# A recurrent update on VectorE or a third chunk on TensorE: the sample tokens of a gated DeltaNet layer

## The reference, cut to what matters

```python
S = S * exp(g_t); kv = k_t @ S                     # sample tokens, one by one
S = S + outer(k_t, (v_t - kv) * b_t); o_t = q_t @ S
o = rmsnorm(o, norm_w) * silu(z)                   # both kinds of tokens
```

## Time and profile before

| | |
|---|---|
| time, median of 3 runs | 2902.24 us (2901.11 to 2912.59) |
| the profiled execution | 2906.3 us, span 2904.3 us |
| mean granted TensorE clock | 0.918 |
| busy: PE, DVE, ACT, POOL | 2579.0, 1751.0, 1083.1, 1654.3 us |
| span by stretches: prologue; GDN loop; last GDN pass | 0 to 135; 135 to about 1304; to about 1388 us |
| granted clock in the GDN loop; in the output projection after it | 0.88; 1.00 |
| chain that ended last, first two shares | issue 35%, POOL 30% |

### The profile page before, as it was taken

One profiled execution on the slowest core, in us unless ns is written; L12 is line 12 of the kernel. 1 busy time (PEld: TensorE's weight loads), 2 busy tenths in 40 slices (PEclk: granted clock), 3 DMA queues, 4 the chain that ended last, 5 costly groups with the idle time before them and its releaser, 6 DMA issues.

```text
span 2904.3 us, 58389 instructions
## 1 busy us (share of the span) xinstructions
PE 2579.0 (89%) x21022; PEld 2378.3 (82%) x21022; DVE 1751.0 (60%) x3882; ACT 1083.1 (37%) x1752; POOL 1654.3 (57%) x2236
## 2 busy tenths in 40 slices
PE   6888889889888898898999898788988899799998
PEld 5877888778778787887999898777977788699987
DVE  5767667676776766767321415777777676823242
ACT  5433333333333333333333434343433434433343
POOL 4534434343444443433788676566755676597765
PEclk8988889889888898988999998999999999899999
DMA  4333333233333322333545345446654565264433
GB/s 179 117 117 118 130 117 117 89 115 116 117 117 117 131 96 95 121 112 116 187 152 176 103 155 194 155 150 202 209 168 139 187 219 182 100 214 143 155 116 119
DMA packets 126773, 410.86 MB, mean 141 GB/s; under 512 B 21344, under 2 KB 37984, under 8 KB 122112
## 3 DMA queue, kind: packets, MB, share of 16 engines
q1 hardware_dynamic: 81216, 295.75, 30.3%
q10 hardware_dynamic: 45504, 114.38, 11.3%
HBM read 363.47 MB, written 46.61 MB: 141 GB/s over the span
## 4 chain that ended last, share of the span: by engine, by line
issue 35%; POOL 30%; PE 22%; DVE 11%; ACT 2%; DMA 0%; POOLq 0%; ACTq 0%; DVEq 0%
POOL wl L313 30%; PE psj L336 6%; PE psj L338 6%; PE psj L337 6%; DVE arena L1271 4%; DVE arena L1269 2%; DVE arena L1561 1%; ACT arena L1109 1%; PE psA L676 1%; PE psE L343 1%; PE psE L631 1%; DMA arena<-s_rows_d 0%; DVE arena L1634 0%; DVE arena L1632 0%; PE psA L343 0%
## 5 line engine op out<-in xcount | busy, mean ns | idle before, releaser
L313 POOL TENSOR_TENSOR wl<-ring,wh 128x256 fp32r<-128x256 f32 x2232 | 1654.1, 777 | 1227.3 <-ACT wh L727 1226.4
L336 PE MATMUL psj<-xh,wh 128*128 128x288 f32 x4400 | 1416.7, 322 | 49.0 <-DVE xl L1208 20.0
L337 PE MATMUL psj<-xl,wh 128*128 128x288 f32 x4400 | 1335.4, 304 | 0.0
L338 PE MATMUL psj<-xh,wl 128*128 128x288 f32 x4400 | 1329.4, 302 | 0.0
L336 PEld LDWEIGHTS psj<-xh,wh 128*128 128x128 f32 x4400 | 861.9, 196 | 135.4 <-issue 99.4
L337 PEld LDWEIGHTS psj<-xl,wh 128*128 128x128 f32 x4400 | 865.4, 197 | 8.5 <-issue 3.9
L338 PEld LDWEIGHTS psj<-xh,wl 128*128 128x128 f32 x4400 | 863.6, 196 | 0.0
L727 ACT ACTIVATE wh<-ring 128x1024 fp32r<-128x1024 f32 x558 | 564.5, 1056 | 241.3 <-PE psj L338 214.8
L1271 DVE SCALAR_TENSOR_TENSOR arena<-arena 128x256 f32<-128x256 f32 (+1 forms) x672 | 325.0, 549 | 2.6
L795 ACT ACTIVATE arena<-psj 128x256 f32<-128x256 f32 x112 | 42.9, 383 | 403.1 <-PE psj L338 401.0
L1542 DVE TENSOR_TENSOR arena<-Y,arena 128x288 f32<-128x288 f32 x32 | 14.6, 458 | 163.1 <-ACT arena L988 162.4
(11 more groups left out here) (283 smaller groups left out, 3097.3 us busy)
## 6 DMA issues: line engine op xcount, KB each, us to landing
ring<-weights_d SPq DMA_DIRECT2D x558, 512.0 KB, 3.3
h<-gstate_d ACTq DMA_DIRECT2D x16, 1024.0 KB, 7.3
gst_s_d<-h ACTq DMA_DIRECT2D x16, 1024.0 KB, 3.9
h<-sstate_d ACTq DMA_DIRECT2D x32, 512.0 KB, 6.4
sst_s_d<-h ACTq DMA_DIRECT2D x32, 512.0 KB, 5.1
arena<-g_rows_d ACTq DMA_DIRECT2D x16, 864.0 KB, 4.5
arena<-s_rows_d ACTq DMA_DIRECT2D x8, 1152.0 KB, 9.8
h_spill_d<-h ACTq DMA_DIRECT2D x2, 2304.0 KB, 7.8
```

Of the source, the lines that this page charges most:

```text
L313: ins = pool.tensor_tensor(wl[:, s, n:n + 2], ring[:, s, n:n + 2], wh[:, s, n:n + 2].bitcast(F32), ALU.subtract)
L336: pe.matmul(out, w_h, xh[:, kt, :], start=(kt == 0), stop=False)
L337: pe.matmul(out, w_h, xl[:, kt, :], start=False, stop=False)
L338: mm = pe.matmul(out, w_l, xh[:, kt, :], start=False, stop=(kt == KT - 1))
```

## The change

The 32 sample tokens become a third chunk of the chunked rule, with the mask "same sequence, and token not later". The sample part on VectorE is replaced by small products on TensorE, and outputs of both kinds come out with tokens on partitions, so that the norm's sum runs along the columns of one partition.

- TensorE, step 0: k^T k and k^T q of the sample tokens (psE) instead of a transpose. Step 3: two transposes of k spread by sequence, and the read-out of the states as 16 products of 256 columns, k into rows 0 to 31 and q into rows 32 to 63 of psD. Steps 6, 7, 10: the inverse of the 32 x 32 matrix from two factors. Step 19: the sample v to tokens. Step 23: the new values, step 27: the outputs. Step 31: all eight updates of the states, in four banks. Step 36: six transposes of the normed outputs (psE, psF), after g_on. Step 39: the sums for the next q and k, in psA and psB.
- `gdn_ready(m, e)` holds three waits ahead of the projection of a step: g_as before step 6, g_bs before step 10, the scaled new values before step 27.
- VectorE: the exponents of pairs, pair products and `gdn_sample` go. New are the masks of k and q by sequence, some operations on 32 x 32, the row sum of squares (768 columns), the scaling of outputs (g_on), and the two products to Y, which now stand among the updates of the states.
- ScalarE: the decay exponents of GDN and of SSD as Relu of (cumulated g of the column's token as a bias, minus the row), with scale -1 in the Exp; squares out of PSUM; one root of 6 columns; the roots of the next q and k stand ahead of the stores of the states.
- Prologue: a few masks, 20 small products, one copy more.

The diff, cut to its core:

```diff
+            def gdn_ready(m, e):
+                if e == 6:
+                    pe.wait_ge(S("g_as"), m + 1)
+                if e == 10:
+                    pe.wait_ge(S("g_bs"), m + 1)
+                if e == 27:
+                    pe.wait_ge(S("g_sample_act"), m * 4 + SMP_ACT["vnds"])
...
                 if e == 3:
-                    pe.wait_ge(S("g_pr"), m + 1)
-                    col_sum(psD[:, 0:2 * NPAIR], ga["PR"])
+                    pe.wait_ge(S("g_mk"), m + 1)
+                    for r in range(2):
+                        mm = pe.transpose(psF[:, r * P:(r + 1) * P], gMK[:, 4 * r:4 * r + 4, :], ident)
+                    mm.then_inc(S("g_sample_pe"), 1)
                     pe.wait_ge(S("g_st_in"), m * 16 + 16)
                     for b in range(DEC_B):
-                        for j in range(2):
-                            at = 160 + 16 * b + 8 * j
-                            mm = halves(psD, slice(at, at + 8), gS[:, b, j, :], gKN[:, 0:2, SEQ + b:T:DEC_B])
-                    mm.then_inc(S("g_smp"), 1)
+                        for n in range(2):
+                            mm = pe.matmul(psD[NS * n:NS * n + NS, 0:2 * P], (gMK, gMQ)[n][:, b, :], gS[:, b, :, :],
+                                           start=(b == 0), stop=(b == DEC_B - 1))
+                    mm.then_inc(S("g_sample_pe"), 1)
...
+                if e == 31:
+                    pe.wait_ge(S("g_sample_act"), m * 4 + SMP_ACT["kmc"])
+                    pe.wait_ge(S("g_ot"), m + 1)
+                    for r in range(2):
+                        for g in range(4):
+                            rows = slice(NS * g, NS * g + NS)
+                            mm = pe.matmul((psA, psB, psC, psD)[g][:, r * 256:(r + 1) * 256], gKM[rows, r, :],
+                                           gVNDS[rows, :], start=True, stop=True)
+                    mm.then_inc(S("g_sp"), 1)
+                if e == 36:
+                    pe.wait_ge(S("g_on"), m + 1)
+                    for j in range(2):
+                        for c in range(NC):
+                            at = j * SEQ + c * CH
+                            pe.transpose(psE[:, at:at + CH], gON[:, 2 * c + j, :], ident)
+                    for j in range(2):
+                        mm = pe.matmul(psF[:, NS * j:NS * (j + 1)], gON[NS:2 * NS, 4 + j, :],
+                                       ident[NS:2 * NS, NS:2 * NS], start=True, stop=True)
+                    mm.then_inc(S("g_ont"), 1)
+                if e == 39 and more:
+                    pe.wait_ge(S("g_su"), m * 4 + 2)
                     gdn_norm(m + 1)
...
 (ScalarE, start of a pass)
-                act.activation(ga["DT"], ga["DT"], ACT.Exp)
-                act.activation(ga["DEC"], ga["DEC"], ACT.Exp).then_inc(S("g_dte"), 1)
+                for c in range(NC):
+                    for j in range(2):
+                        act.activation(gDT[:, 2 * c + j, :], gR[:, j, 0, c * CH:(c + 1) * CH], ACT.Relu,
+                                       bias=gcc[:, 1, c, j:j + 1], scale=-1.0)
+                for j in range(2):
+                    ins = act.activation(gDTS[:, j, :], gR[:, j, 0, SEQ:T], ACT.Relu, bias=gscc[:, 1, j:j + 1],
+                                         scale=-1.0)
+                ao.link(ins)
+                act.activation(ga["DT"], ga["DT"], ACT.Exp, scale=-1.0).then_inc(S("g_dte"), 1)
...
 (VectorE, in the inversion: level lv)
                     if lv < CONV_W:
                         v_tap(lv)
+                    if lv == 1:
+                        dve.wait_ge(S("g_sample_pe"), m * 7 + SMP_PE["sqs"])
+                        dve.tensor_tensor(gBS[:, :, :], bc(ident[0:NS, 0:NS], 1, 2),
+                                          psD[0:NS, 256:256 + 2 * NS].rearrange("p (j t) -> p j t", j=2), ALU.add) \
+                            .then_inc(S("g_bs"), 1)
...
 (VectorE, end of a pass; states(g) updates the sequences g and 4 + g)
+                dve.wait_ge(S("g_osq"), m + 1)
+                dve.tensor_reduce(ga["OS"], gSQO[:, :, :], AXIS.X, ALU.add).then_inc(S("g_oss"), 1)
+                dve.wait_ge(S("g_sp"), m + 1)
+                states(0)
+                dve.wait_ge(S("g_rs2"), m + 1)
+                do.link(dve.reciprocal(ga["OR"], ga["OR"]))
+                dve.tensor_tensor(gON[:, 0:4, :], psF[:, :].rearrange("p (u t) -> p u t", u=4),
+                                  bc(ga["OR"][:, 0:4], 2, P), ALU.mult)
+                dve.tensor_tensor(gON[NS:2 * NS, 4:6, :], gOT[:, :, :], bc(ga["OR"][NS:2 * NS, 4:6], 2, P), ALU.mult) \
+                    .then_inc(S("g_on"), 1)
+                states(1)
...
 (ScalarE, SSD layer, before each of the two Exps)
+                    for hh in range(HPG):
+                        ins = act.activation(sDT[:, hh, :], sR2[:, hh, c * CH:(c + 1) * CH], ACT.Relu,
+                                             bias=scc[:, 1, c, hh:hh + 1], scale=-1.0)
```

More of the change, by code:

```diff
@@ L20 @@
 ACT = mybir.ActivationFunctionType
+AXIS = mybir.AxisListType
 P = 128
@@ L77 @@
 N_PRM = C_SND + 2 * SX * SG
-G_DVE_LINKS, S_DVE_LINKS = 34, 27
+SMP_PE = {n: i + 1 for i, n in enumerate(("kmt", "smp", "ast", "sqs", "esp", "us", "osm"))}
+SMP_ACT = {n: i + 1 for i, n in enumerate(("kmc", "asc", "qs", "vnds"))}
+G_DVE_LINKS, S_DVE_LINKS = 19, 27
 ARENA = 15900
@@ L446, in gdn_mix @@
                     new_values(0)
+                if e == 23:
+                    pe.wait_ge(S("g_es"), m + 1)
+                    pe.wait_ge(S("g_rss"), m + 1)
+                    for j in range(2):
+                        mm = pe.matmul(psA[:, j * P:(j + 1) * P], gES[:, j, :, :], gVBS[:, j, :], start=True, stop=True)
+                    mm.then_inc(S("g_sample_pe"), 1)
                 if e == 24:
@@ L508, in _ @@
                 for c in range(NC):
-                    src = HRG[0:GV, (7, 3, 4, 5)[n], c * CH:(c + 1) * CH]
+                    src = HRG[0:GV, (7, 6, 4, 5)[n], c * CH:(c + 1) * CH]
                     at = (n * NC + c) * GV
                     mm = pe.transpose(psD[:, at:at + GV], src, ident[0:GV, 0:GV])
+            for n in range(5):
+                src = HRG[0:GV, (7, 6, 4, 8, 5)[n], SEQ:T]
+                for g in range(4):
+                    mm = pe.matmul(psD[NS * g:NS * g + NS, 256 + n * GV:256 + (n + 1) * GV], src, ident[0:GV, 0:GV],
+                                   start=True, stop=True)
             mm.then_inc(S("g_ccol"), 1)
@@ L892, in gdn_body @@
                         u = 2 * c + j
[L893 to L894 removed]
+                        act.activation(gVB[:, u, :], psB[:, u * P:(u + 1) * P], ACT.Copy,
+                                       scale=gcc[:, 0, c, j:j + 1])
+                for j in range(2):
+                    ins = act.activation(gVBS[:, j, :], psE[0:NS, 256 + j * P:256 + (j + 1) * P], ACT.Copy,
+                                         scale=gscc[0:NS, 0, j:j + 1])
                 ins.then_inc(S("g_vb"), 1)
@@ L1437, in gdn_body @@
                 less_q(1, 5)
-                dve.wait_ge(S("g_cv"), m + 1)
-                for piece in range(1, 6):
-                    gdn_sample(piece, m)
+                dve.wait_ge(S("g_sample_pe"), m * 7 + SMP_PE["smp"])
+                dve.wait_ge(S("g_vb"), m + 1)
+                dve.wait_ge(S("g_dtx"), m + 1)
+                for j in range(2):
+                    ins = dve.scalar_tensor_tensor(gVBS[:, j, :], psD[0:NS, j * P:(j + 1) * P], gscc[0:NS, 2, j:j + 1],
+                                                   gVBS[:, j, :], ALU.mult, ALU.add)
+                ins.then_inc(S("g_rss"), 1)
                 if not full:
@@ L1459, in gdn_body, with states @@
                     take_out(T_O1, 1)
-                for i in range(4):
-                    dve.wait_ge(S("g_sp"), m * 4 + i + 1)
-                    for b in (2 * i, 2 * i + 1):
+                def states(g):
+                    bank = (psA, psB, psC, psD)[g]
+                    for r in range(2):
+                        b = 4 * r + g
                         for j in range(2):
-                            at = (b % 2) * 256 + j * P
+                            at = r * 256 + j * P
                             ins = dve.scalar_tensor_tensor(gS[:, b, j, :], gS[:, b, j, :],
@@ L1477, in gdn_body @@
                     .then_inc(S("g_y"), 1)
+                states(2)
+                states(3)
                 if full:
```

281 lines of the change are left out of this document (135 added, 146 removed).

## The result

The changed kernel takes **2821.45 us** (median of 4 runs, 2816.62 to 2824.59) against 2901.99 (4 runs) for the kernel before: ratio 0.9716, 95% interval 0.97 to 0.9732. The profiled execution took 2822.21 us, span 2820.4, mean granted clock 0.95. The forecast was 2830, the range 2765 to 2905: the time lies in it, and "faster by over 0.5%" had the chance 0.66.

The account below looks back on a forecast made before the run. TensorE's in-order queue, with its waits and the lower clock behind them, was taken to bound the kernel. 79.4 against 84.03 us a pass, 15 times, is -69; with -9 SSD and +1.5 prologue, 2906.3 becomes 2829.8, said as 2830 (2765 to 2905).

Parts of the forecast that it names:

- Part I: Steps 31 to 0 of a pass, 29.45 us before: 17.3 work, 2.2 wait, 2.0 clock, 21.5 us (19.5 to 24).
- The term of 2.0 for the clock: Behind the wait for normed outputs at step 36: 2.0 us lost to a lower clock, between bounds 0 and 4.3.
- The prediction's own bracket: How long TensorE may wait: clock kept at 1.00 after a 2.56 us wait, 0.67 after 2.75.
- Part II: Steps 0 to 7 of a pass, 17.53 us before, claimed to become 13.7 us (11.8 to 17.5).
- Part III: Steps 7 to 31, 37.05 us before, to become 44.2 us (40 to 46), with 3.7 wait before step 10.
- the signs that were to show it: Waits: step 10, 3 to 4 us; step 36, 2 to 3; step 6, about 1; Part III clock under 0.95.
- four signs of being wrong: Clock 1.00 after step 10; wait there under 1 us; read-out 7 us; normed outputs over 9 us after step 31.
- SSD: SSD layer: exponents leaving VectorE remove waits of 1.14 us a group, 9 us gained in all (0 to 12).
- (a): Clock kept after both new waits, at steps 36 and 10: 83 us less, 2747; chance 0.12.
- (b): Clock low for a whole stretch after both new waits, steps 36 and 10: 54 us more, 2884; chance 0.16.
- (c): Read-out of the states: two 32-wide tiles don't overlap as four do, +3.85 a pass, 58 us, 2888; chance 0.07.
- (d): Normed outputs for step 36 come late, 14.4 us instead of 8.2: 128 us more, 2958; chance 0.13.

Follow-up runs that it names:

- run 9: Changed kernel with the BS products at step 12 instead of 10 and state stores ahead of the next q/k roots, read-out still at step 3: 2725.77 us, ratio 0.9393.
- run 5: Kernel before, with the GDN prompt decay exponents as Relu on ScalarE and VectorE's pair products ahead of the sample-pair exponents: 2822.2 us, ratio 0.9726.
- run 3: Changed kernel with ScalarE's stores of the states ahead of the next q and k roots: 2792.05 us, ratio 0.9625.
- run 8: Changed kernel with BS products at step 12, state stores ahead of the next roots, and the read-out of the states at step 5: 2742.59 us, ratio 0.9434.
- run 1: Changed kernel with the wait for g_bs and its two small products moved from step 10 to step 12: 2750.42 us, ratio 0.9484.
- run 2: Changed kernel with the SSD layer's decay exponents back on VectorE, GDN untouched: 2833.98 us, ratio 0.9769.
- run 6: Changed kernel with the 16 read-out products reordered, all keys and then all queries instead of in turn: 2856.89 us, ratio 0.9839.
- run 4: Kernel before, with only the GDN prompt decay exponents moved to ScalarE as Relu: 2863.56 us, ratio 0.9866.
- run 10: run 9 with the transposes of the normed outputs at step 38 instead of 36 and VectorE's last state updates earlier: 2707.32 us, ratio 0.9331.
- run 7: Changed kernel with the read-out of the states moved from step 3 to step 17: 2873.38 us, ratio 0.9895.

## Why the prediction was right, step by step

**Part I** (21.5 predicted, 19.80 measured). The wait for the normed outputs: predicted 2.2, since g_on at 8.2 and TensorE ready at 6.0; measured 1.70, with g_on 8.0 us after step 31 and TensorE ready at 6.3. The work without a wait was predicted as 17.3 and is 18.10, 0.8 too little. The term of 2.0 for the clock was wrong in this pass: it stayed at 1.00. So -0.5 - 2.0 + 0.8 = -1.7: two errors hide a third. In run 9 both occur, behind 1.70 and 1.69 us of the same wait:

```profile
361.90:372.00 10.10, 10.08 (x72) 9.67 (x73) 8.33 (x17) 3.15 (x6) 3.43 (x5) 1.00 0.50 183
434.10:444.20 10.10, 10.09 (x60) 9.58 (x61) 6.88 (x17) 3.15 (x6) 1.99 (x3) 0.83 0.54 184
```

0.17 of 10.1 us is 1.7 lost in one pass and nothing in another. The size 2.0 was about right for a pass in which it happens; in the changed kernel it happens in 3 of 15, which makes 0.3 a pass. The prediction's own bracket had put this wait on the side that is kept, and against it I took the 2.0. The bracket itself (kept behind 2.56, lost behind 2.75) did not hold either: the clock was lost behind 1.69 in run 9, and kept over 9 us behind 2.40 in run 5.

**Part II** (13.7 predicted, 17.28 measured): the largest error. At full clock the read-out takes 3.65 us (run 3; predicted 3.85), but in the changed kernel the clock falls inside it: 17.28 x 0.10 = 1.7, a loss that the prediction had put at nothing here. The states land later than I counted, so that the wait was 2.34, not 1.0 (+1.3): the load took 8.7 us from issue to landing (median of the 16), where the earlier trace rows have 6.7 in the pass that I read. The wait of 0.95 for the masked keys I had missed; VectorE, which masks them, waits itself for the rows of g, that leave the same queue:

```profile
DVE arena L1404 <- DMA arena<-g_rows_d: 53.7, 16, 3.7
```

 The wait of 0.9 for g_as did not come, as TensorE was later by all of this; in run 8, where it was not, it is there, 0.90 us. 13.7 + 1.7 + 1.3 + 0.95 - 0.9 = 16.8 of 17.3. Run 3 shows the queue as the cause of most: with the stores first, 2 us a pass come back.

**Part III** (44.2 predicted, 42.45 measured). The wait for g_bs was predicted as 3.7 and is 3.71 us; run 1 takes it away. The clock cost 42.45 x 0.04 = 1.7, not 3.5: it fell only after the wait was over and was low for about 3.4 us (0.62 in the first 3.05 us, 0.85 in the next 3.5). That both old waits of 1.1 us would go was right, and so were the 2.2 for products and copies as a whole: 37.05 - 2.2 + 3.7 + 1.7 + 2.2 = 42.45. (Three times the 0.61 of the earlier trace rows are 1.8, not 1.7 with two tiny products on top.)

The errors of the three parts, -1.7, +3.6 and -1.7, cancel to +0.1 (79.53 in this pass against 79.4). The total was right to 0.3% partly by luck; of the four waits that came I had three in the right place and two in about the right size, and a fifth did not come; of the clock behind them I had only the loss at step 10, at twice its size. Of the signs that were to show it, these came otherwise: the wait before step 36 is 1.70 and not 2 to 3 us, there is none before step 6, parts I and II are 9.9 and not 12 us shorter, and part III has a clock of 0.96, where I wanted under 0.95. None of the four signs of being wrong came. **SSD**: 9 predicted, 12.5 measured (run 2), since the wait is longer than 1.14 in one group (5.0). **Prologue**: 1.5 and 1.1.

**The rivals.** (a) the clock kept after both waits: half true, it was kept at step 36 in 12 of 15 passes and lost at step 10 in all. (b) low for a whole stretch: no. (c) 32-wide tiles that don't overlap: excluded by the 3.65 us of run 3; run 6 shows what it would have cost. (d) g_on late: excluded, 8.0 us. The Trainium skill's rule that relu belongs on VectorE ("ScalarE: Activation LUTs", Rules for kernel authors) did not pay here: the move to ScalarE gained 38 us in the kernel before (run 4), and the way back cost 12.5 in the SSD layer (run 2). The Relus of 128x128:

```profile
404.63 1.28 ACT L926 ACTIVATE arena<-arena 128x128 f32<-128x128 f32 x4 [0.45 <-DVE arena L1407]
```

0.32 us each, against 0.74 on VectorE beside GpSimd. Alone VectorE needs 0.28 (the median of L1561), so one instruction for one the rule is not refuted; what decided was whose queue the work stood on. Relu needed no table load of its own: the one of 1.28 stands ahead of the first Relu, from 402.89, while ScalarE waits for VectorE anyway, and serves the Exp as well.

**What stays open.** Why the clock falls in one pass and not in the next behind the same wait. Behind the 3.7 us of the changed kernel it fell each time, in the pass read 0.7 us later; behind 2.31 in run 4 it fell, behind 2.40 in run 5 it did not, and behind 0.53 with 0.90 in run 8 it did both. The length of a wait does not decide it alone. No run takes part I apart, the largest gain of all: how much of it is the state products, the norm's sums or the order of the queue is not shown.

## What to carry to other kernels

Where one engine runs a written-out order, price a change by what stands on that engine's queue, and try the order first: moving existing work gave 71, 29 and 18 us (runs 1, 3, 10) and 41 us in the old kernel (run 5 against run 4), beside 80 for the change of method, and busy totals of the other engines told nothing. Price each wait twice, its own length and the clock that may fall behind it, and don't count a removed wait before looking at the one that it hid (runs 5 and 7). Work taken off an engine beside a contending one frees less than its duration, since what follows moves into the contention (run 4).

## What the runs showed of the hardware that I had not expected

- Four operations of VectorE with two SBUF inputs of 128x64 took 0.52 us alone and 2.82 us beside GpSimd, a factor of 5; the four on 128x256 of the earlier trace rows differ by 2.6. Beside GpSimd one operation took about the same whatever its size, 0.71 us for 128x64, 0.74 for 128x128 and 0.77 for 128x256, close to the 0.78 of one GpSimd instruction (mean of L313), so small operations lose most.
- Products in 32-wide tiles of two columns: 3.65 us at full clock for 32 passes of 256 columns in turn, 7.93 (clock 0.78) one side after the other.
- The load of the states took longer to landing in the changed kernel than before, with the same bytes and the same queue. Medians of the 16 loads, before and then after:

```profile
h<-gstate_d ACTq DMA_DIRECT2D x16, 1024.0 KB, 7.3
```

```profile
h<-gstate_d ACTq DMA_DIRECT2D x16, 1024.0 KB, 8.7
```

- In one trace (run 8) the granted clock stayed full behind 0.53 and 0.90 us of waiting after narrow products in the early passes and fell in each later one; it stayed full behind 2.40 us after projection products (run 5).
